# First three projections of a layer cut into two contraction halves, with their weights loaded before the second half of the modulation weights

## The chip, the core and the metric

The kernel runs on one core of one Trainium2 chip. The metric is the device time of one execution in microseconds. Three runs of the kernel before gave 792.9, 792.96 and 793.29 us, so their median is 792.96 us. The engines are named as in the profile: PE is TensorE (PEld its weight loads), DVE is VectorE, ACT is ScalarE, POOL is GpSimd, SP is SyncE, which here only issues the big transfers. All data is 32-bit floating point.

## The reference, cut to what matters

Two layers, each on 128 context tokens and 128 latent tokens of width 1024. The part that the change touches is the beginning of a layer:

```
m = silu(cond) @ w_mod + b_mod            # 6 x 1024 values per condition: shift, scale, gate, ...
h = rmsnorm(x, g_mix) * (1 + scale) + shift
aq, ak, av, mq, mk, mv, mo, mi, mf = split(h @ w_in)      # one combined input projection
group A: bidirectional mLSTM from mq, mk, mv, gates mi, mf, output gate mo
group B: grouped-query attention from aq, ak, av
x = x + gate1 * (concat(attention, mLSTM) @ w_out)
x = x + gate2 * moe(rmsnorm(x, g_ffn) * (1 + scale2) + shift2)   # 16 experts, 512 wide
```

Shift and scale of a feature need all 1024 rows of w_mod, but only the columns of that feature. A projection sums over all 1024 features of h (the contraction); the first 512 features are its first half.

## The kernel before, in words

Tokens lie transposed: a tile of h (hT) has 8 chunks k of 128 features, each with 256 columns, two blocks b of 128 tokens (block 0 context, block 1 latent). Every big weight arrives in pieces of 2 MB (1 MB for akv). They go round a ring of seven slots (ring), in the order of weight_plan(), and the experts use three slots more (beside, over). SP issues the transfers strictly in that order; before each it waits until the last user of the slot has read it (was_read). A wait of SP therefore holds back every later transfer. Small inputs are issued by ACT and POOL; POOL begins with them when the first projection weight (mk) has landed.

Within a layer the shift and scale of the first norm (section 0 of the modulation) are made first. In layer 0 section_rows multiplies four slots of w_mod, each two rows k of 2048 columns, on PE (L639, 16 recorded instructions for one slot); ACT copies the row (L1298), PE turns it (L651), DVE adds the bias and makes 1 + scale (L1591, L1598), and ACT and DVE apply it to the normed tokens (L1341, L1609). Then PE projects in the order mk, mq with the gate columns between its halves, mv, aq, scan and maximum rows, akv, mo (project L764, project_turned L778). A matmul of 512 columns is two recorded instructions.

Section 1 of the modulation (the gate of the mixer) isn't made on PE but summed on DVE: section_sums multiplies each of its four ring slots (blocks 0 to 3, in the file called ("mod", l, 1, i)) by the condition and adds it up (L1676, L1678), four instructions for each block. The table SUM_TURNS says how many blocks are summed at each of three turns: before the scan rows of the mLSTM, after the mq copies, and after gaps(0), the first half of the decay matrix (L1740). Before, layer 0 has three blocks in the first turn, one in the second, none in the third. PE reads the sums right after mo (L729). After that turn DVE empties akv out of PSUM (L1749, L1750), makes gaps(1), the q and k norms and the rotary (L1756 to L1782), the reciprocal of the output gate (L1787) and the weighted scores of the mLSTM (L1796), on which the first state-free matmuls of the mLSTM (own, L892) wait.

The experts follow: eight pairs of experts in a layer, 12 MB each, PE bound to the slots' landing (L1100 gate and up, L1130 down).

Of the kernel before, what the change touches and what calls it, by code (L numbers as in the profile page):

```python
# [105 lines left out]
SECTION_CHUNKS[1, 2], SECTION_CHUNKS[1, 3] = (32, 8), (40, 8)  # L106


def section_slots(l, s):

    return SECTION_CHUNKS[l, s][1] // 4
# [17 lines left out]
BETWEEN = {"mk": (0,), "mq": (1, 2), "mv": (3,)}  # L129
SUM_TURNS = (((0, 1, 2), (3,), ()), ((0, 1, 2), (3,), ()))  # L130


def bank_plan():
# [15 lines left out]
    put(("modrow", 0, 0), 7)  # L149
    put(("modcol", 0, 0), 7)  # L150
    for l in range(DEPTH):
# [10 lines left out]
        put(("gates", l), 4)  # L162
        for g in PROJ:
            for b in range(NB):
                turn((g, b))
        put(("gateT", l), 5)
# [69 lines left out]
def weight_plan():  # L236
# [13 lines left out]
    for i in range(section_slots(0, 0)):  # L250
        put(("mod", 0, 0, i))
    for l in range(DEPTH):
        for g in PROJ:
            put((g, l))
            for i in BETWEEN.get(g, ()):
                put(("mod", l, 1, i))
# [16 lines left out]
def build(nc, t):  # L273
    banks, weights = bank_plan(), weight_plan()
    with ExitStack() as ctx:
# [132 lines left out]
        first_read, last_half = sem("first_read"), sem("last_half")  # L408
        sum_step = sem("sum_step")
# [86 lines left out]
        def _(sp):  # L496
# [51 lines left out]
            load_section(0, 0, 0)  # L548
# [3 lines left out]
            load_section(0, 0, 1, 2, 3)  # L552
            for l in range(DEPTH):
                for g, (c0, width) in PROJ.items():
                    load((g, l), w_in[l, :, :, c0:c0 + width], width)
                    if g in BETWEEN:
                        load_section(l, 1, *BETWEEN[g])
# [53 lines left out]
        def _(pe):  # L611
# [33 lines left out]

            def section_columns(l, s):
# [64 lines left out]
            for l in range(DEPTH):  # L711
                bank = begin(("rows", l))
                done(("rows", l), pe.transpose(bank[:, 0:ROWS_L], rowsin[:, l, :], ident[0:ROWS_L, 0:ROWS_L]))
            pe.wait_ge(x_in, 16 * NB)
            for r in range(4):
# [5 lines left out]
                done(("x", r), mm)  # L721

# [10 lines left out]
            for l in range(DEPTH):  # L733
                if l == 0:
                    pe.wait_ge(cond_silu, 1)
                    section_rows(0, 0, 0)
                else:
                    warm((("mk", 0), l), 4)
                norm_parts(l, 0)
                if l == 0:  # L740
                    norm_parts(l, 1)
                    section_rows(0, 0, 1)
                norm_total(l, 0)
                if l == 0:
                    norm_total(l, 1)
                    section_rows(0, 0, 2, 3)
                    warm((("mk", 0), l), 3)
                    section_columns(0, 0)
                    warm((("mk", 0), l), 6)
                else:  # L750
# [4 lines left out]
                def project(g, which=range(NB), fresh=False):  # L755
                    _, width = PROJ[g]
                    w = landed((g, l))[:, 0:KD * width].rearrange("p (k n) -> p k n", k=KD)
                    for b in which:
                        bank = begin(((g, b), l))
                        for k in range(KD):  # L760
                            if fresh:
                                ready, n = (h_v, HV_STEPS) if k % 2 else (h_a, HA_STEPS)
                                pe.wait_ge(ready, n * l + 4 * b + k // 2 + 1)
# [4 lines left out]
                        done(((g, b), l), mm)  # L768

                def project_turned(g, which):  # L770

                    w = landed((g, l)).rearrange("p (k n) -> p k n", k=KD)
                    for i in which:
                        bank = begin(((g, i), l))
                        for j in range(2):
                            h = 2 * i + j
                            for k in range(KD):
                                mm = pe.matmul(bank[:, j * TOK:(j + 1) * TOK], w[:, k, h * MD:(h + 1) * MD], hT[:, k, :],  # L778
                                               start=(k == 0), stop=(k == KD - 1))
                        done(((g, i), l), mm)  # L780
# [46 lines left out]
                project("mk", fresh=True)  # L827
# [1333 lines left out]
```

## Time and profile before

| what | value |
|---|---|
| median of three runs | 792.96 us |
| profiled execution, its own time | 794.9 us |
| span in it | 793.0 us |
| PE busy | 759.5 us, 96% |
| DVE busy | 329.3 us, 42% |
| ACT busy | 158.2 us, 20% |
| bytes moved | 289.41 MB, 365 GB/s over the span |
| granted clock, mean | 0.996 |

The profiled execution is 1.9 us longer than its span. Busy shares are a mean over stages: PE is busy nearly everywhere after the first projection starts, and transfers run at full rate except at the start, in a gap before layer 0's mixer ends and in one in layer 1. What counts for a change of the first stage is which wait ends last in it, and whether that time survives the later waits.

### The profile page before, as it was taken

How to read it: one execution, taken by the hardware profiler on the slowest of the kernel's cores; microseconds unless marked ns; L12 is line 12 of the kernel's file. 1: busy time of each engine (PE TensorE's matmuls, PEld its weight loads, DVE VectorE, ACT ScalarE, POOL GpSimd, SP SyncE). 2: the span in 40 equal slices, each digit the busy share in tenths (PEclk: the TensorE clock that was granted, in tenths of full speed). 3: DMA queues.
4: the chain of work that ended last, by engine and by line, in shares of the span. 5: the costliest groups of instructions: out<-in, count | busy, mean ns of one | idle time of the engine just before them, and what ended most of it. 6: DMA issues, size and time to landing. Idle time of an engine off the chain costs nothing.

```text
span 793.0 us, 10913 instructions
## 1 busy us (share of the span) xinstructions
PE 759.5 (96%) x4683; PEld 401.3 (51%) x4683; DVE 329.3 (42%) x534; ACT 158.2 (20%) x355; POOL 56.6 (7%) x69
## 2 busy tenths in 40 slices
PE   3799999999999999999899999999899999999997
PEld 2265556786534433444245646688653444344423
DVE  0279566714323232123228965772431323213223
ACT  2301114602212012020012111361221201102001
POOL 0040052101100000000000004200110000000000
PEclk9999999999999999999999999999999999999999
DMA  8999907999999999999999970579889999999993
GB/s 346 403 378 374 375 7 295 413 362 424 426 420 424 423 421 425 426 419 423 422 407 407 380 301 0 218 289 397 326 328 400 427 426 418 424 426 419 426 421 152
DMA packets 49858, 289.41 MB, mean 365 GB/s; under 512 B 3401, under 2 KB 5761, under 8 KB 23697
## 3 DMA queue, kind: packets, MB, share of 16 engines
q1 hardware_dynamic: 48080, 285.30, 88.6%
q0 software_dynamic: 1488, 3.31, 1.2%
q8 instruction: 39, 0.64, 0.3%
q10 hardware_dynamic: 240, 0.08, 0.0%
q14 instruction: 11, 0.08, 0.0%
HBM read 286.31 MB, written 2.37 MB: 364 GB/s over the span
## 4 chain that ended last, share of the span: by engine, by line
PE 83%; DMA 13%; DVE 2%; SPq 1%; ACT 1%; issue 0%; ACTq 0%; DVEq 0%
PE ps L1100 22%; PE ps L764 16%; PE ps L1130 12%; DMA ring<-in_w_e_up 9%; PE ps L1014 7%; PE ps L1084 4%; DMA ring<-in_w_in 4%; PE ps L778 4%; PE ps L639 3%; PE ps L1145 2%; PE ps L1112 1%; PE ps L1155 1%; PE ps L892 1%; PE ps L917 1%; PE ps L947 1%; DVE xT L1654 1%
## 5 line engine op out<-in xcount | busy, mean ns | idle before, releaser
L1100 PE MATMUL ps<-ring,xe 128*64 128x512 f32 x688 | 151.8, 594 | 4.0 <-DMA ring<-in_w_e_up 4.0
L764 PE MATMUL ps<-ring,hT 128*128 128x512 f32 (+1 forms) x320 | 128.7, 564 | 2.0 <-DMA ring<-in_w_in 2.0
L1100 PEld LDWEIGHTS ps<-ring,xe 128*64 128x64 f32 x688 | 48.5, 137 | 105.3 <-issue 99.8
L764 PEld LDWEIGHTS ps<-ring,hT 128*128 128x128 f32 x320 | 62.1, 196 | 65.2 <-issue 59.5
L1130 PE MATMUL ps<-ring,ex 128*32 128x512 f32 x736 | 92.0, 594 | 0.2 <-issue 0.2
L1995 DVE COPY ye<-ps 64x512 f32<-64x512 f32 (+1 forms) x28 | 19.3, 689 | 164.2 <-PE ps L1130 164.1
L1014 PE MATMUL ps<-hT,ring 128*128 128x256 f32 x256 | 57.1, 381 | 0.0
L1979 DVE RECIPROCAL ex<-ex 128x512 f32<-128x512 f32 x16 | 53.6, 3353 | 0.6
L1130 PEld LDWEIGHTS ps<-ring,ex 128*32 128x32 f32 x736 | 26.0, 110 | 52.1 <-issue 49.4
L1977 DVE TENSOR_SCALAR ex<-ex 128x512 f32<-128x512 f32 x16 | 6.8, 427 | 109.4 <-ACT ex L1528 109.4
L1014 PEld LDWEIGHTS ps<-hT,ring 128*128 128x128 f32 x256 | 48.0, 190 | 7.2 <-issue 0.8
L1100 PE MATMUL ps<-beside,xe 128*64 128x512 f32 x208 | 46.2, 594 | 0.0
L1528 ACT ACTIVATE ex<-ps 128x512 f32<-128x512 f32 x16 | 9.6, 597 | 143.4 <-PE ps L1100 143.4
L1130 PE MATMUL ps<-beside,ex 128*32 128x512 f32 x224 | 35.3, 594 | 2.0 <-issue 2.0
L1678 DVE SCALAR_TENSOR_TENSOR pT<-ring,cT,pT 128x2048 f32<-128x2048 f32 x14 | 32.9, 2348 | 5.6 <-DMA ring<-in_w_mod 5.6
L1678 DVE SCALAR_TENSOR_TENSOR sideways<-ring,cT,sideways 128x2048 f32<-128x2048 f32 x14 | 32.9, 2347 | 0.0
L1084 PEld LDWEIGHTS ps<-lists,hT 128*128 128x128 f32 x256 | 29.7, 192 | 5.8 <-issue 4.9
L639 PE MATMUL ps<-ring,cT 128*32 128x512 f32 (+1 forms) x320 | 31.6, 525 | 0.6 <-DMA ring<-in_w_mod 0.6
L1084 PE MATMUL ps<-lists,hT 128*128 128x128 f32 x256 | 31.6, 278 | 0.1
L1544 ACT ACTIVATE ye<-ps 64x512 f32<-64x512 f32 (+1 forms) x28 | 16.6, 592 | 68.7 <-PE ps L1130 68.6
L1521 ACT ACTIVATE xe<-ps 128x512 f32<-128x512 f32 x32 | 19.1, 597 | 54.0 <-PE ps L1084 54.0
L1100 PEld LDWEIGHTS ps<-beside,xe 128*64 128x64 f32 x208 | 14.6, 137 | 30.0 <-issue 29.9
(272 smaller groups left out, 803.6 us busy)
## 6 DMA issues: line engine op xcount, KB each, us to landing
ring<-in_w_mod SPq DMA_DIRECT2D x24, 2048.0 KB, 19.1
ring<-in_w_e_up SPq DMA_DIRECT2D x23, 2048.0 KB, 20.0
ring<-in_w_e_gate SPq DMA_DIRECT2D x20, 2048.0 KB, 22.3
ring<-in_w_e_down SPq DMA_DIRECT2D x19, 2048.0 KB, 23.2
ring<-in_w_in SPq DMA_DIRECT2D x10, 2048.0 KB, 23.4
beside<-in_w_e_gate SPq DMA_DIRECT2D x8, 2048.0 KB, 25.5
beside<-in_w_e_down SPq DMA_DIRECT2D x7, 2048.0 KB, 19.8
beside<-in_w_e_up SPq DMA_DIRECT2D x5, 2048.0 KB, 18.1
```

The lines of the kernel that those rows point to most:

```text
L639: mm = pe.matmul(bank[32 * g:32 * g + 32, 0:width], cT[:, c:c + 32], w[:, k, g * width:(g + 1) * width], start=(c == 0), stop=(c == NB * ( ...
L764: mm = pe.matmul(bank[:, 0:width], hT[:, k, b * P:(b + 1) * P], w[:, k, :], start=(k == 0), stop=(k == KD - 1))
L778: mm = pe.matmul(bank[:, j * TOK:(j + 1) * TOK], w[:, k, h * MD:(h + 1) * MD], hT[:, k, :], start=(k == 0), stop=(k == KD - 1))
L1014: mm = pe.matmul(bank[:, j * TOK:(j + 1) * TOK], w[:, k, c:c + P], cat[:, k, :], start=(k == 0), stop=(k == KD - 1))
L1084: mm = pe.matmul(bank[:, c:c + P], htok[:, b, 2 * i + k, :], pick[:, b, 4 * q:4 * q + 4, :].rearrange("p e c -> p (e c)"), start=True, sto ...
L1100: mm = pe.matmul(bank[PLACES * j:PLACES * j + PLACES, :], xe[:, k, c:c + PLACES], w[:, j, i, :], start=(k == 0), stop=(k == KD - 1))
L1130: mm = pe.matmul(bank[32 * g:32 * g + 32, :], hidT[:, k, c:c + SLOTS], w[j][:, k, half * 512:(half + 1) * 512], start=(k == 0), stop=(k == ...
L1521: act.activation(xe[:, 2 * i:2 * i + 2, :].rearrange("p k (e b s) -> p b (k e) s", e=4, b=NB), bank[:, :].rearrange("p (b n s) -> p b n s" ...
L1544: ins = act.activation(ye[r, plane, 0:512], bank[r, :], ACT.Copy)
L1678: ins = dve.scalar_tensor_tensor(modsum[b], w[:, k % 2, :], one, modsum[b], ALU.mult, ALU.add)
L1979: dve.reciprocal(ex[:, :], ex[:, :]).then_inc(silu_step, 1)
L1995: ins = dve.tensor_copy(ye[r, plane, 512:1024], bank[r, :])
```

## The change

Section 0 of layer 0 is cut by features: part -1 is shift and scale of features 0 to 511 (two slots, all 1024 rows of w_mod), part 0 those of features 512 to 1023. feature_rows multiplies a slot with 32 matmuls of 128 columns in place of 8 of 512. mk, mq and mv of layer 0 are loaded and multiplied in two halves of the contraction. Weights of the first halves stand ahead of part 0 of w_mod, and tokens and constants ahead of every weight. Section 1 of layer 0 is loaded behind akv and mo, its sums on DVE are taken as 1, 1 and 2 blocks. Projections keep their partial sums in PSUM between the halves (mv moved to banks 4 and 5, gates to 6, gateT to 7). POOL's small inputs start when the first half of mk has landed. The last scatter of layer 0's experts stands behind the branch for spilled tokens.

```diff
+HALVED = ("mk", "mq", "mv")
-BETWEEN = {"mk": (0,), "mq": (1, 2), "mv": (3,)}
-SUM_TURNS = (((0, 1, 2), (3,), ()), ((0, 1, 2), (3,), ()))
+BETWEEN = ({"akv": (0, 1), "mo": (2, 3)}, {"mk": (0,), "mq": (1, 2), "mv": (3,)})
+SUM_TURNS = (((0,), (1,), (2, 3)), ((0, 1, 2), (3,), ()))
...
+            load_features(-1)
+            for g, landed in zip(HALVED, front_in):
+                if weights[g, 0][0] == RING - 1:
+                    taken(sp, ("x", 0), ("x", 1), ("x", 2), ("x", 3))
+                load_rows(g, slice(0, KD // 2), landed)
+            load_features(0)
+            for g in HALVED:
+                load_rows(g, slice(KD // 2, KD), slot_landed[weights[g, 0][0]])
...
+            def feature_rows(s, *which):
+                bank = begin(("modrow", 0, s)) if 0 in which else ps[banks["modrow", 0, s][0]]
+                for v in which:
+                    w = landed(("mod", 0, s, v)).rearrange("p (k n) -> p k n", k=KD)
+                    for k in range(KD):
+                        for g in range(4):
+                            mm = pe.matmul(bank[32 * g:32 * g + 32, v * P:(v + 1) * P], cT[:, NB * k:NB * k + 32],
+                                           w[:, k, g * P:(g + 1) * P], start=(k == 0), stop=(k == KD - 1))
...
+            pe.wait_ge(ones_set, 3)
+            warm(("x", 0), 12)
             pe.wait_ge(const_in, 16)
-            pe.wait_ge(ones_set, 3)
-            pe.wait_ge(rows_in, 16 * ROW_LOADS * DEPTH)
...
+                    front, back = range(0, KD // 2), range(KD // 2, KD)
+                    project("mk", fresh=True, ks=front)
+                    project_turned("mq", range(NB), front)
+                    feature_rows(0, 0, 1)
+                    project("mv", (0,), ks=front)
+                    section_columns(0, 0)
+                    project("mv", (1,), ks=front)
+                    project("mk", fresh=True, ks=back)
+                    project_turned("mq", (0,), back)
+                    gates()
+                    project_turned("mq", (1,), back)
+                    gate_rows()
+                    project("mv", ks=back)
...
-                if l + 1 < DEPTH:
-                    scatter_pair(PAIRS - 1, 0, KD)
                 with pe.If(limit[0] > SLOTS):
...
-                if l + 1 == DEPTH:
-                    scatter_pair(PAIRS - 1, 0, KD)
+                scatter_pair(PAIRS - 1, 0, KD)
...
+                    taken(dve, (("ssq1", 1), l))
+                    scaled(sq, 1, 0, KD)
+                    dve.wait_ge(xr_ready, n + 3)
+                    for s in (-1, 0):
+                        feature_columns(s)
+                        for b in range(NB):
+                            modulate(l, sq, b, (4 * s + 5, 4 * s + 7))
...
-            pool.wait_ge(slot_landed[weights["mk", 0][0]], 16)
+            pool.wait_ge(front_in[0], 16)
```

In feature_rows the four values of g are the four strips of 32 rows of the PSUM bank; in a partial project_turned a matmul of zeros clears the bank first (L831 of the changed kernel), since two heads share it.

PE, before, from the first slot of w_mod to the first projection of layer 0 (ring holds the weights, cT the two conditions, hT the modulated tokens, ps a PSUM bank):

```order
L639 MATMUL ps<-ring,cT 32x512 x8
L676 MATMUL ps<-work,ones 32x128 x16
L639 MATMUL ps<-ring,cT 32x512 x8
L685 MATMUL ps<-rstd,ones 128x128 x2
L639 MATMUL ps<-ring,cT 32x512 x16
L691 MATMUL ps<-zeros 128x512 x3
L651 MATMUL ps<-cst,ring 128x128 x4
L691 MATMUL ps<-zeros 128x512 x6
L764 MATMUL ps<-ring,hT 128x512 x16
L778 MATMUL ps<-hT,ring 128x256 x16
```

PE, changed, from the second slot of part -1 on, with the semaphores that each group waits on:

```order
L685 MATMUL ps<-ring,cT 32x128 [waits slot_landed1]
L685 MATMUL ps<-ring,cT 32x128 x31
L697 MATMUL ps<-cst,ring 128x128 [waits bank_read7]
L818 MATMUL ps<-ring,hT 128x512 [waits h_a,bank_read0,mk_front_in]
L831 MATMUL ps<-zeros 128x512 [waits bank_read2,mq_front_in]
L836 MATMUL ps<-hT,ring 128x256 x8
L685 MATMUL ps<-ring,cT 32x128 [waits slot_landed2,bank_read7]
L685 MATMUL ps<-ring,cT 32x128 [waits slot_landed3]
L818 MATMUL ps<-ring,hT 128x512 [waits bank_read4,mv_front_in]
L818 MATMUL ps<-ring,hT 128x512 [waits bank_read5,mv_front_in]
L818 MATMUL ps<-ring,hT 128x512 [waits h_a,slot_landed4]
L836 MATMUL ps<-hT,ring 128x256 [waits slot_landed5]
```

Before the first projection PE now reads two slots of w_mod in place of four; the other two are read behind the front halves of mk and mq.

DVE, before, from the second turn of sums to the emptying of akv in layer 0 (pT and sideways hold the two running sums, W the decay matrix):

```order
L1678 SCALAR_TENSOR_TENSOR sideways<-ring,cT,sideways 128x2048
L1728 COPY qc<-ps6 128x64
L1740 TENSOR_SCALAR W<-ps4,qc 128x128 x4
L1740 TENSOR_SCALAR W<-ps5,qc 128x128 x4
L1749 COPY qk<-ps0 128x128
L1750 COPY vx<-ps0 128x2x64
L1740 TENSOR_SCALAR W<-ps6,qc 128x128 x4
```

DVE, changed, the same place:

```order
L1826 COPY qc<-ps6 128x64
L1838 TENSOR_SCALAR W<-ps5,qc 128x128 x4
L1776 SCALAR_TENSOR_TENSOR pT<-ring,cT,pT 128x2048 [waits sum_step,slot_landed5]
L1776 SCALAR_TENSOR_TENSOR sideways<-ring,cT,sideways 128x2048 [waits sum_step]
L1776 SCALAR_TENSOR_TENSOR pT<-ring,cT,pT 128x2048 [waits sum_step]
L1776 SCALAR_TENSOR_TENSOR pT<-ring,cT,pT 128x2048 [waits sum_step,slot_landed6]
L1847 COPY qk<-ps 128x128 [waits bank_full2]
L1848 COPY vx<-ps 128x2x64
```

Eight sums (two blocks of four, of which half are listed) now stand between gaps(0) and the emptying of akv, where none stood; the first turn has four in place of twelve.

## Rows read from the trace of the kernel before

**Rows 1.** The page: GB/s in 40 slices of 19.8 us

```profile
GB/s 346 403 378 374 375 7 295 413 362 424 426 420 424 423 421 425 426 419 423 422 407 407 380 301 0 218 289 397 326 328 400 427 426 418 424 426 419 426 421 152
```

**Rows 2.** The chain of waits in order of time: start us, us, what

```profile
5.35 28.75 DMA ring<-in_w_in
34.14 15.70 PE ps L764 x32
49.84 6.91 PE ps L778 x32
...
65.86 27.66 PE ps L764 x64
```

**Rows 3.** Timeline, 15 to 34 us: start us, us, engine, line, instructions, idle before

```profile
18.93 0.61 PE L676 MATMUL ps<-work,ones 128*32 128x128 f32 x16
...
27.48 1.92 PE L639 MATMUL ps<-ring,cT 128*32 128x512 f32 x16 [0.62 <-DMA ring<-in_w_mod]
...
31.31 1.65 ACT L1341 ACTIVATE hT<-work,modc,amp 128x128 f32<-128x128 f32 x4 [1.25 <-DVE amp L1598]
```

**Rows 4.** Stretches, PE alone: us, busy (instructions), granted clock, DMA share, GB/s

```profile
0.00:20.00 20.00, 7.77 (x50) 1.00 0.88 346
20.00:40.00 20.00, 15.80 (x91) 0.91 1.03 399
40.00:60.00 20.00, 20.00 (x82) 1.00 1.03 380
28.00:30.00 2.00, 2.00 (x19) 1.00 1.06 389
36.00:37.00 1.00, 1.00 (x2) 0.50 0.97 391
98.00:99.00 1.00, 1.00 (x4) 0.50 0.04 16
170.00:175.00 5.00, 5.00 (x30) 1.00 0.74 298
416.00:420.00 4.00, 4.00 (x30) 1.00 1.05 396
```

**Rows 5.** Timeline of DVE in layer 0's mixer

```profile
79.14 2.35 DVE L1678 SCALAR_TENSOR_TENSOR pT<-ring,cT,pT 128x2048 f32<-128x2048 f32 x1
81.41 2.35 DVE L1678 SCALAR_TENSOR_TENSOR sideways<-ring,cT,sideways 128x2048 f32<-128x2048 f32 x1
...
95.78 2.16 DVE L1740 TENSOR_SCALAR W<-ps,qc 128x128 f32<-128x128 f32 x8 [1.35 <-PE ps L822]
...
105.61 0.28 DVE L1750 COPY vx<-ps 128x128 f32<-128x128 f32 x1
...
117.17 0.83 DVE L1782 TENSOR_TENSOR qkr<-work 128x640 f32<-128x640 f32 x1
122.45 0.19 DVE L1591 TENSOR_TENSOR modc<-ps,cols 128x32 f32<-128x32 f32 x1 [4.44 <-PE ps L651]
...
125.94 2.42 DVE L1796 TENSOR_TENSOR W<-ps,W 128x512 f32<-128x512 f32 x4
```

**Rows 6.** Timeline of PE in layer 0's mixer

```profile
93.46 0.71 PE L811 MATMUL ps<-cst,prob 64*128 64x64 f32 x8
...
130.81 1.38 PE L892 MATMUL ps<-mv,W 128*128 128x129 f32 x10
```

**Rows 7.** Waits of SP, 140 to 215 us: us in total, times, longest

```profile
SPq L576 <- DMA out_new_state_n<-nst: 20.4, 1, 20.4
```

**Rows 8.** Timeline of POOL, 150 to 210 us

```profile
165.01 0.53 POOL L2113 DMA_DIRECT2D out_new_state_n<-nst  x1
```

**Rows 9.** Timeline of PE, end of layer 0's experts

```profile
377.47 7.07 PE L1130 MATMUL ps<-beside,ex 128*32 128x512 f32 x64 [1.99 <-issue]
...
392.42 3.65 PE L1100 MATMUL ps<-ring,xe 128*64 128x512 f32 x16 [0.86 <-DMA ring<-in_w_e_up]
397.29 3.22 PE L1100 MATMUL ps<-ring,xe 128*64 128x512 f32 x14 [1.22 <-DMA ring<-in_w_e_up]
```

More of the change, by code:

```diff
@@ L161, in bank_plan @@
         put((("ssq1", 1), l), 5)
-        put(("gates", l), 4)
+        put(("gates", l), 6 if l == 0 else 4)
         for g in PROJ:
             for b in range(NB):
-                turn((g, b))
-        put(("gateT", l), 5)
+                if l == 0 and g == "mv":
+                    put((("mv", b), 0), 4 + b)
+                else:
+                    turn((g, b))
+        put(("gateT", l), 7 if l == 0 else 5)
         put(("scanT", l), 6)
@@ L248, in put @@
         order.append(slot)
-    for i in range(section_slots(0, 0)):
-        put(("mod", 0, 0, i))
+    for s in (-1, 0):
+        for i in range(section_slots(0, s)):
+            put(("mod", 0, s, i))
+    for g in HALVED:
+        put((g, 0))
     for l in range(DEPTH):
         for g in PROJ:
-            put((g, l))
-            for i in BETWEEN.get(g, ()):
+            if l > 0 or g not in HALVED:
+                put((g, l))
+            for i in BETWEEN[l].get(g, ()):
                 put(("mod", l, 1, i))
@@ L551, in _, with load_features, load_rows @@
                 sp.dma_start(xtok[:, b, :], t[name][0]).then_inc(x_in, 16)
[L552 removed]
+            def load_features(s):
+                for i in range(section_slots(0, s)):
+                    slot, _, _ = weights["mod", 0, s, i]
+                    c = KD * P * i + WB * (s + 1)
+                    sp.dma_start(ring[:, slot, :].rearrange("p (k n) -> p k n", k=KD), w_mod[0, :, :, c:c + WB]).then_inc(slot_landed[slot], 16)
+            def load_rows(g, ks, landed):
+                c0, width = PROJ[g]
+                sp.dma_start(ring[:, weights[g, 0][0], :].rearrange("p (k n) -> p k n", k=KD)[:, ks, :],
+                             w_in[0, :, ks, c0:c0 + width]).then_inc(landed, 16)
+            load_features(-1)
[4 more added lines that the diff above has]
+            load_features(0)
+            for g in HALVED:
+                load_rows(g, slice(KD // 2, KD), slot_landed[weights[g, 0][0]])
             for l in range(DEPTH):
                 for g, (c0, width) in PROJ.items():
[L555 to L557 removed]
+                    if l > 0 or g not in HALVED:
+                        load((g, l), w_in[l, :, :, c0:c0 + width], width)
+                    if g in BETWEEN[l]:
+                        load_section(l, 1, *BETWEEN[l][g])
                 for sec in later_sections(l)[1:-1]:
@@ L721, in _ @@
                 done(("x", r), mm)
+            pe.wait_ge(rows_in, 16 * ROW_LOADS * DEPTH)
+            for l in range(DEPTH):
+                bank = begin(("rows", l))
+                done(("rows", l), pe.transpose(bank[:, 0:ROWS_L], rowsin[:, l, :], ident[0:ROWS_L, 0:ROWS_L]))
             def section_sums(l, s):
```

127 lines of the change are left out of this document (80 added, 47 removed).

## The prediction

> **What bounds the kernel now.** I read the page's slices first, then the chain of waits, then the timelines of the stretches that the chain crosses. The transfers run at 346 to 425 GB/s for most of the span, with a hole at 99 to 119 us (7 GB/s) and one in layer 1 [rows 1]. The chain begins with a transfer: the wait for the first projection weight lasts 28.75 us, mk starts on PE at 34.14, and from there the chain stays on PE through mk, mq, mv, aq [rows 2]. So the first 34 us are bound by bytes, and behind them PE is bound by its own work. PE's later idle time that a transfer ends is 1.99, 0.86 and 1.22 us at the end of layer 0's experts, 4.1 together [rows 9]: PE and the transfers run nearly level there, which matters for what survives of an early start. The hole at 99 to 119 us shows that a start of PE some microseconds earlier meets weights that can also come earlier.
>
> **The sum is made against the profiled execution**: span 793.0, own time 794.9 us, 1.9 above the median 792.96. Each term below is a shift, negative for earlier, and carries over to the median unchanged.
>
> **Term 1, the start of mk.** Before, the fourth slot of w_mod landed at 27.48 [rows 3]. Asked for by then were four slots of 2.10 MB, 1.05 MB of tokens and 0.15 of constants and rows, 9.6 MB; moved were 20 us x 346 GB/s + 7.48 us x 399 = 9.9 MB [rows 4]. For mk, landed at 34.14 with 11.7 MB asked for, 12.6 were moved. So landing lags the queue by 0.3 to 0.9 MB. Changed: constants, tokens and two slots are 5.4 MB, with the lag 5.7 to 6.3 MB, which counted back from 6.92 MB at 20 us with some 0.4 MB in a microsecond is 17.0 to 18.4; I take 18.0, since pieces of 2 KB are now the rule. Then the second slot's rows on PE. Their form isn't in the trace; the nearest is the norm's 32x128 matmul, 16 recorded instructions in 0.61 us, 0.57 when nothing overlaps at the end, 0.036 each [rows 3]. A slot is 32 matmuls or 64 instructions: 2.3 us (the 32x512 form of before took 1.92 for a slot [rows 3], that is the lower bound; twice the row, 4.6, the upper). End at 20.3. From the end of the last rows (29.40) to the first modulated chunk (31.31 + 0.41) before were 2.3 us, through copy, transposes, bias and scale [rows 3]; the same again gives 22.6, and the six zero matmuls behind the transposes fill PE to about 23.0. The first half of mk needs 6.4 + 0.9 = 7.3 MB, there at 21. The norm of both blocks goes through ACT before that: the tokens no longer stand behind 2.1 MB of weights and come some 5 us earlier, so it is hidden under the slots of w_mod. So mk starts at 23.0 in place of 34.14: **-11.1 us**.
>
> **Term 2, work added on PE before the end of mv.** The matmuls of the three projections stay the same in number. New behind the start of mk are the two slots of part 0, 2 x 2.3 = 4.6 us, their transposes 0.35, and two zero matmuls that clear the banks of mq, 0.25 each (a recorded instruction of a 512-column matmul takes 13.83 / 32 = 0.43, the upper bound): 5.45 us. Must PE wait for part 0? Asked for up to its second slot are 5.4 + 3 x 1.05 + 2 x 2.10 = 12.7 MB, with the lag 13.6, and with 0.6 MB of the small inputs, which now start at 21 in place of 34.14, 14.2 MB. At 399 GB/s that is 38.2 us, at 380 GB/s [rows 4] 39.2. PE wants the slot at 23.0 + 6.9 (half of mk) + 7.5 (half of mq, 6.91 to 7.1 [rows 2], and the clearing) + 2.3 = 39.7. No wait, but little room: every 5% of rate is 1 us. The back halves (1.05 MB each) land before 46, PE takes mk's at 49. Before, the granted clock was at the lower level (0.50, that is 1.2 GHz) soon after the start, as at 36 to 37 [rows 4], and mk took 15.70 us where 32 instructions of mv or aq take 27.66 / 2 = 13.83 [rows 2]: 1.9 us. I leave this loss in, as if the first heavy stretch always paid it. Shift at the end of mv and at the scan columns: -11.1 + 5.45 = -5.65, term 2 **+5.45 us**.
>
> **Term 3, sums on DVE.** Before, aq ended and the scan columns were at 93.46, gaps(0) on DVE at 95.78 to 97.9, akv copied by 105.9 [rows 5, 6]. Changed, eight sums of 2.26 us (81.41 - 79.14) stand behind gaps(0): 18.1 us, then the four copies at 1.0: 19.1 in place of 8.0, so DVE is 11.1 us later against PE. Their slots land in time: SP issues them as mq and mv are read, near 64 and 72, and they are wanted at 90 and 99. Behind the sums are queued akv's copies, gaps(1), norms, rotary, the reciprocal and the weighted scores, for which PE waits with own. What slack has that queue? 4.44 us idle before L1591, which waited for PE, and between the first half of the weighted scores (125.94 + 1.21) and own at 130.81 another 3.66 [rows 5, 6]: 8.1. 11.1 - 8.1 = **+3.0 us** for PE. Bounds: 0 if the queue closes up elsewhere (the POOL squares and ACT's root are asked for later than before), 11.1 if no slack can be used. In the same stretch ACT copies the modulation row only behind the q and k roots; PE reaches it at 112.6, waits about 3 us, and that wait is part of the same 3.0, not more.
> The first turn has four sums in place of twelve. It ends when the first block has landed (about 61) and 7.0 us later, at 68, level with the logarithm that the scan waits for (PE's gate rows end near 65), and aq, 13.8 us on PE, covers the scan either way: 0.
>
> **Term 4, the queue before the experts.** SP waited 20.4 us for new_state_n, issued by POOL at 165.01 and landed 9.1 later [rows 7, 8]; meanwhile the queue ran dry for a while (298 GB/s, 0.74 busy at 170 to 175) [rows 4]. Changed, six slots (section 2 and w_out) can load before the modulation's columns are turned, where before three could; fewer bytes are then left over in front of the experts. Three slots of experts' weights wait behind new_state_n, 6.3 MB or 16 us of transfer, which before ran to about 190 and would now start while the queue is empty and end before PE frees the next slot: I put the lead at 1.6 us on top of the shift, of the 4.1 which PE lost to transfers at the end of the experts [rows 9]. **-1.6 us**, bounds 0 and -4.1.
>
> The scatter behind the branch: layer 1 has it in this order and starts it without a gap, 0. The zero matmuls at the very start stand ahead of the tokens, when PE has nothing to do: 0.
>
> Sum: -11.1 + 5.45 + 3.0 - 1.6 = -4.25. Span 788.75, own time 790.65, on the scale of the median **788.7 us**.
>
> **A rule on the clock.** At 416 to 420 mk of layer 1 starts right behind zero matmuls at the granted 1.00, while mk of layer 0 started behind 2 us of idleness and fell to 0.50 soon after [rows 4]. The Trainium skill says, in TensorE: Matmul & The Clock Gate, section Part 1: The HAM clock gate, that the half rate is the resting state and steady work releases it; by that rule the changed start, filled with zero matmuls to its last microsecond, keeps the full rate. The row at 98 to 99 (0.50 in the middle of dense work [rows 4]) goes against so simple a reading. Its result is the first rival.
>
> **A rule on pieces.** w_mod's pieces become 2 KB in place of 8 KB; while mk, also of 2 KB pieces, landed, the rate was 389 GB/s at a DMA share of 1.06, against 399 over the whole 20 us [rows 4]. The Trainium skill, DMA: Bandwidth & Descriptors, section Specifications, gives 512 B as enough for full rate, so by it the smaller pieces cost nothing; by the row, 3% of the 8 MB or 0.6 us, of which only the first half is on the path.
>
> **The rivals.**
> 1. No low clock at mk: 1.9 us less, 786.8; with the whole 4.1 of term 4 as well, 784.3. For it: the zero matmuls up to the start. Against: the 0.50 at 98.
> 2. The 4.44 us of DVE's slack can't be used, because the columns of the modulation slip with ACT's queue and DVE still waits for them: -4.25 + 4.44 = +0.2, 793.2. Or less: a new low clock (1.9) in PE's 3 us of waiting and no lead in term 4 (1.6): 792.2. For it: ACT's row copy stands behind DVE's reductions. Against: DVE itself reaches the columns at 121.8, by my times 5 us after PE has turned them.
> 3. Slower: the eight sums set PE's pace in full. Place: between gaps(0) and own in layer 0. Price 11.1 with no slack at all: -5.65 + 11.1 - 1.6 = +3.85, 796.8. It decides once more than 8.1 + 4.25 = 12.3 us of delay reach own, or the slack is under 3.9. For it: a chain over DVE, POOL, ACT and back. Against: the idle rows.
> 4. Small inputs and short pieces make part 0 late: each microsecond behind 39.7 costs one; 44 is break-even. It would take 300 GB/s between 20 and 44; the slices there say 374 and more [rows 1]. It widens the range only.
>
> **Chances.** Forecast (787.7 to 790.8) 0.42; rival 1 0.30; rival 2 0.18; rivals 3 and 4 0.10. A measurement here tells 0.2% (1.6 us) from no change, so faster means under 791.4: 0.42 + 0.30 + a quarter of rival 2 = 0.76; same 0.15; slower 0.09. Range 785.0 to 792.8; the likeliest case alone, 787.7 to 790.8.
>
> **What the changed profile would show.** mk starts at 22 to 24.5, and 64 instructions of the new row form take 2 to 3 us. No wait over 1 us before part 0. Scan columns at 87 to 89. DVE without a gap from gaps(0) to the weighted scores, and PE idle 2 to 4 us between mo and own. own at 127 to 129. Waits at the experts' end under 3 us. I would be wrong if mk started after 26, if PE waited for DVE by more than 6 us, or if the shift at own didn't reach the end of the span.

## The result: slower, and the profile after

| | before | changed |
|---|---|---|
| median | 792.93 us (792.17 to 793.29, 4 runs) | 800.5 us (799.67 to 801.25, 4 runs) |
| profiled execution | 794.9 us, span 793.0 | 799.67 us, span 797.9 |
| granted clock, mean | 0.996 | 0.99 |

The ratio is 1.0093, 95% interval 1.008 to 1.0106. The prediction was 788.7 us, faster; the kernel became 7.6 us slower. The two profiled executions stand 4.9 us apart (the one of before lies 2 us above its median, that of the changed kernel is the fastest of its four), so positions below explain 4.9 of the 7.6. Most of the other 2.7 lies in the profiled execution of before. Experiment 12 (the kernel before with one scatter moved) runs the same code up to the end of layer 0's experts, and its profile shows that code at the higher clock:

```profile
33.60 14.00 PE L764 MATMUL ps<-ring,hT 128*128 128x512 f32 x32 [1.81 <-DMA ring<-in_w_in]
...
92.06 0.71 PE L811 MATMUL ps<-cst,prob 64*128 64x64 f32 x8
...
127.73 2.06 PE L892 MATMUL ps<-mv,W 128*128 128x129 f32 x16
```

```profile
98.00:99.00 1.00, 1.00 (x6) 1.00 0.00 0
```

There mk takes 14.00 us, not 15.70, akv and mo (the last L764, 64 instructions) 20.91, not 22.59, and the weighted matmuls of the mLSTM (own) start at 127.73, not 130.81. Against this profile the changed kernel's first w_out matmul comes 7.2 us late (161.88 to 154.65), close to the 7.6 of the medians. Experiment 1, whose PE code is also that of before, takes 14.00 and 20.91 too. So one profile in three was at the lower clock at these two places, and that execution is the base of the prediction and of its rows. What decided it no run shows: zero matmuls and a wait of 1.7 to 2.0 us stand ahead of mk in all three. Below, "against the undisturbed profile" means against experiment 12 up to the first w_out matmul.

The start did what it should. PE timeline of the changed kernel, from the second slot of part -1 to part 0 (start us, us, engine, line, out<-in, instructions, idle before and what ended it):

```profile
19.52 1.96 PE L685 MATMUL ps<-ring,cT 128*32 128x128 f32 x64 [0.60 <-DMA ring<-in_w_mod]
...
23.63 7.11 PE L818 MATMUL ps<-ring,hT 128*128 128x512 f32 x16
...
38.00 1.96 PE L685 MATMUL ps<-ring,cT 128*32 128x128 f32 x64
41.23 0.97 PE L685 MATMUL ps<-ring,cT 128*32 128x128 f32 x28 [1.27 <-DMA ring<-in_w_mod]
```

mk starts at 23.63 where it started at 34.14 [rows 2], the new row form takes 1.96 us, and part 0 waits for 1.27. The start itself varies: in eleven profiles of kernels that share it, mk starts at 23.2 to 25.7, while the scan columns come at 86.8 to 87.7 in all of them. The trouble is on DVE. Its timeline, first turn of sums to the third:

```profile
65.97 1.29 DVE L1774 TENSOR_SCALAR pT<-ring,cT 128x2048 f32<-128x2048 f32 x1 [17.16 <-DMA ring<-in_w_mod]
...
73.15 0.42 DVE L1788 SCALAR_TENSOR_TENSOR prob<-prob 64x256 f32<-64x256 f32 x1
...
88.25 2.34 DVE L1776 SCALAR_TENSOR_TENSOR sideways<-ring,cT,sideways 128x2048 f32<-128x2048 f32 x1
90.51 0.21 DVE L1826 COPY qc<-ps 128x64 f32<-128x64 f32 x1
92.08 2.20 DVE L1838 TENSOR_SCALAR W<-ps,qc 128x128 f32<-128x128 f32 x8 [1.35 <-PE ps L882]
94.19 2.34 DVE L1776 SCALAR_TENSOR_TENSOR pT<-ring,cT,pT 128x2048 f32<-128x2048 f32 x1
```

DVE waits 17.16 us for the first block, and from 65.97 it works nearly without a gap: scan, second turn to 90.5, qc, gaps(0), third turn. PE's scan columns are ready at 87.9, and PE waits for qc:

```profile
87.18 0.71 PE L871 MATMUL ps<-cst,prob 64*128 64x64 f32 x8
90.87 2.31 PE L882 MATMUL ps<-prob,cst 32*128 32x256 f32 x16 [2.99 <-DVE qc L1826]
...
128.57 0.63 PE L947 MATMUL ps<-cst,qkr 128*128 128x128 f32 x4 [3.43 <-DVE qkr L1880]
...
133.31 3.69 PE L967 MATMUL ps<-mv,W 128*128 128x129 f32 x16 [0.86 <-DVE W L1894]
```

Here the scan columns answer to L811 and own to L892 of [rows 6]: 93.46 became 87.18, but 130.81 became 133.31 (92.06 and 127.73 in the undisturbed profile), with 3.43 us of waiting for the turned queries and keys and 0.86 for the weighted scores in front. Between them the end of DVE's queue:

```profile
112.29 0.28 DVE L1847 COPY qk<-ps 128x128 f32<-128x128 f32 x1
...
113.09 2.15 DVE L1838 TENSOR_SCALAR W<-ps,qc 128x128 f32<-128x128 f32 x8
...
117.32 4.03 DVE L1859 TENSOR_TENSOR qkr<-qk,qk_r 128x640 f32<-128x640 f32 x2 [0.63 <-ACT qk_r L1375]
...
124.14 1.61 DVE L1877 TENSOR_TENSOR work<-qkr,cst 128x160 f32<-128x160 f32 x4
125.79 2.64 DVE L1880 TENSOR_TENSOR qkr<-work 128x640 f32<-128x640 f32 x1
128.35 0.18 DVE L1668 TENSOR_TENSOR modc<-ps,cols 128x32 f32<-128x32 f32 x1
128.56 3.35 DVE L1885 RECIPROCAL og<-og 128x512 f32<-128x512 f32 x1
131.83 2.42 DVE L1894 TENSOR_TENSOR W<-ps,W 128x512 f32<-128x512 f32 x4
```

L1880 is L1782 of [rows 5]: 0.83 us became 2.64. The 4.44 us of idleness before modc are gone, as forecast. POOL meanwhile:

```profile
115.38 5.28 POOL L2192 TENSOR_TENSOR W<-W,cst 128x1024 f32<-128x1024 f32 x2
...
124.07 1.67 POOL L2195 TENSOR_SCALAR og<-og 128x512 f32<-128x512 f32 x1
125.56 2.18 POOL L2200 TENSOR_TENSOR kw<-mk,qc 128x512 f32<-128x512 f32 x2
```

kw runs beside L1880; before, kw came at 121.29, when DVE was idle. Stretches of the changed kernel, PE alone (from:to, length in us, PE busy (instructions), granted clock, DMA share, GB/s):

```profile
4.00:24.00 20.00, 15.07 (x199) 0.91 1.03 382
28.00:40.00 12.00, 11.96 (x105) 1.00 1.04 357
92.00:96.00 4.00, 4.00 (x16) 0.57 0.50 211
132.00:136.00 4.00, 3.14 (x18) 0.50 1.01 420
```

In the same stretches before, 4 to 24 and 28 to 40, transfers ran at 417 and 393 GB/s. The granted clock stays at the higher level under mk (1.00 at 28 to 40). That isn't shown to be a gain of the change, since the undisturbed profile has 1.00 there too, against 0.50 at 36 in [rows 4]. It is at the lower level behind each of the two long waits for DVE, but a wait isn't its only companion: in the profiled execution of before it was 0.50 at 98 behind 0.41 us of waiting.

### The profile page after: what moved, and what is told of

Read it like the earlier page. It is cut to its first block, busy times and chain, and to the rows that moved or that the text cites. A ratio compares the mean times of both kernels' runs of the same rounds, so it can differ in the third digit from the quotient of the medians.

```text
span 797.9 us, 11328 instructions
## 1 busy us (share of the span) xinstructions
PE 765.4 (96%) x4882; PEld 408.9 (51%) x4889; DVE 332.2 (42%) x536; ACT 157.4 (20%) x356; POOL 57.4 (7%) x69
## 4 chain that ended last, share of the span: by engine, by line
PE 73%; DMA 12%; DVE 9%; SPq 2%; issue 2%; ACT 1%; ACTq 0%; DVEq 0%
PE ps L1175 22%; PE ps L1205 12%; PE ps L818 10%; DMA ring<-in_w_e_up 9%; PE ps L1089 7%; PE ps L1159 4%; DMA ring<-in_w_mod 3%; PE ps L836 3%; PE ps L671 2%; PE ps L1220 2%; DVE pT L1776 2%; DVE sideways L1776 2%; SPq L573 1%; PE ps L967 1%; PE ps L1187 1%
## 5 line engine op out<-in xcount | busy, mean ns | idle before, releaser
L818 PE MATMUL ps<-ring,hT 128*128 128x512 f32 (+1 forms) x320 | 127.1, 556 | 0.0
L818 PEld LDWEIGHTS ps<-ring,hT 128*128 128x128 f32 x320 | 61.0, 193 | 61.4 <-issue 58.7
L1175 PEld LDWEIGHTS ps<-beside,xe 128*64 128x64 f32 x208 | 14.6, 137 | 30.0 <-issue 29.9
L2187 POOL TENSOR_TENSOR qkr<-qk 128x640 f32<-128x640 f32 x4 | 5.0, 1250 | 341.9 <-DVE vx L1848 341.9
## 6 DMA issues: line engine op xcount, KB each, us to landing
ring<-in_w_e_gate SPq DMA_DIRECT2D x20, 2048.0 KB, 23.3
ring<-in_w_e_down SPq DMA_DIRECT2D x19, 2048.0 KB, 23.2
```

Of the source, the lines that this page charges most:

```text
L818: mm = pe.matmul(bank[:, 0:width], hT[:, k, b * P:(b + 1) * P], w[:, k, :], start=(k == 0), stop=(k == KD - 1))
L1175: mm = pe.matmul(bank[PLACES * j:PLACES * j + PLACES, :], xe[:, k, c:c + PLACES], w[:, j, i, :], start=(k == 0), stop=(k == KD - 1))
```

## The experiments

Each ratio is against runs of the kernel before on the same chip, with its 95% interval. Times of different experiments come from different chips, so the ratios compare better. The theory throughout: the summing turns make DVE late, and PE pays. The rivals were the transfers, POOL beside DVE, and the clock.

**1. The table alone.** The kernel before with one line changed:

```diff
-SUM_TURNS = (((0, 1, 2), (3,), ()), ((0, 1, 2), (3,), ()))
+SUM_TURNS = (((0,), (1,), (2, 3)), ((0, 1, 2), (3,), ()))
```

> The kernel before with layer 0's sums taken as 1, 1 and 2 blocks, nothing else. Theory (the sums behind gaps(0) and what DVE and POOL do to each other behind them cost more than the start gave): akv copied near 117 in place of 106, own near 136 in place of 130.8, 3 to 8 us slower, 796 to 801. Rival (the loss comes from the new start and the transfers, DVE's slack of 8.1 takes the sums as far as forecast): own at most 3 us later, 793 to 796.

799.79 us, ratio 1.0101 (1.0082 to 1.0121). One line of the change, without the early start, costs what the whole change costs. DVE and PE there:

```profile
119.83 3.99 DVE L1761 TENSOR_TENSOR qkr<-qk,qk_r 128x640 f32<-128x640 f32 x2 [0.63 <-ACT qk_r L1303]
...
128.27 2.64 DVE L1782 TENSOR_TENSOR qkr<-work 128x640 f32<-128x640 f32 x1
```

```profile
131.06 0.93 PE L872 MATMUL ps<-cst,qkr 128*128 128x128 f32 x4 [1.94 <-DVE qkr L1782]
...
135.79 2.03 PE L892 MATMUL ps<-mv,W 128*128 128x129 f32 x16 [0.34 <-DVE W L1796]
```

The same two long instructions, the same two waits, and one more, of 1.64 us for ACT's og at 120. own is 5.0 us later than in the profile before, 8.1 later than in the undisturbed one, which fits the 7.5 us of the medians.

**2. The third turn made cheap.** In the changed kernel layer 0's third turn works on 64 of its 2048 columns, so part of the mixer's gate is left out; the transfers stay. The akv and mo of the next two expectations are one stretch on PE, L818 with 64 instructions.

```diff
+                                c = slice(0, 64 if l == 0 and which == SUM_TURNS[0][2] else 2048)
-                                    ins = dve.scalar_tensor_tensor(modsum[b], w[:, k % 2, :], one, modsum[b], ALU.mult, ALU.add)
+                                    ins = dve.scalar_tensor_tensor(modsum[b][:, c], w[:, k % 2, c], one, modsum[b][:, c], ALU.mult, ALU.add)
```

> The changed kernel with the eight sums of layer 0's third turn on 64 of 2048 columns (leaves out most of two blocks of the sum). Theory: DVE is free at gaps(1) when akv comes, own comes near 125, 7 to 10 us less than the changed kernel, 790.5 to 793.5. Rival (sums aren't the cause): under 3 us less.

793.51 us, ratio 1.0011 (1.0 to 1.0023): 6.5 to 7 us of the change's cost are back. What keeps it from the forecast is the wait for qc, which stands ahead of the third turn and is still there, with the lower clock behind it (3.78 us for what takes 2.00 at the higher, then 23.50 for akv and mo in place of 20.91); own comes at 129.99 where 125 was expected:

```profile
91.06 3.78 PE L882 MATMUL ps<-prob,cst 32*128 32x256 f32 x16 [3.02 <-DVE qc L1827]
```

**3. Second and third turn made cheap.** As 2, with more of the gate left out:

```diff
+                                c = slice(0, 64 if l == 0 and which != SUM_TURNS[0][0] else 2048)
```

> The changed kernel with the sums of layer 0's second and third turns on 64 of 2048 columns (leaves out most of three blocks of the sum). In the run with only the third turn short, PE still waited 3.0 us for DVE at 91, the maximum rows and akv and mo then took 1.8 and 2.7 us more than at the full clock. Theory (DVE's late second turn makes that wait, and the clock falls behind it): no wait at 91, akv and mo at 20.8, own near 124, 786 to 788. Rival (the clock falls there whatever happens): only the 3 us go, 789.5 to 791.

788.59 us, ratio 0.995 (0.9934 to 0.9965).

```profile
88.31 2.00 PE L882 MATMUL ps<-prob,cst 32*128 32x256 f32 x16 [0.41 <-DVE qc L1827]
...
122.86 2.06 PE L967 MATMUL ps<-mv,W 128*128 128x129 f32 x16
```

The wait for qc and the low clock behind it are gone, as the theory says, though 788.59 lies a little outside its 786 to 788 and below the rival's 789.5. own stands 8.0 us earlier than in the profile before and 4.9 earlier than in the undisturbed one; the medians differ by 4.4. So the early start is worth 4 to 5 us once DVE is out of the way. The two later turns cost 10.5 us at own (133.31 against 122.86) and 12 in the medians: 7 by the third turn (experiment 2) and 5 by the second, which ends too late for qc.

**4. kw held back.** POOL starts kw only behind the rotary, so that it doesn't run beside L1880:

```diff
                 taken(pool, ("scanT", l), (("mk", 0), l))
+                pool.wait_ge(qk_ready, NB * l + 2)
```

> The changed kernel with POOL's weighted keys (kw) held until both blocks of q and k are ready. Theory (DVE's last instruction of the rotary took 2.64 us in place of 0.83 because POOL computed beside it): it is back at 0.83, own 1.8 us earlier, 798.5 to 799. Rival (its length comes from elsewhere): 2.6 us stays, 800 to 801.

797.02 us, ratio 1.0054 (1.0037 to 1.0071).

```profile
126.92 0.82 DVE L1880 TENSOR_TENSOR qkr<-work 128x640 f32<-128x640 f32 x1
```

```profile
127.89 0.63 PE L947 MATMUL ps<-cst,qkr 128*128 128x128 f32 x4 [1.62 <-DVE qkr L1880]
...
132.63 2.02 PE L967 MATMUL ps<-mv,W 128*128 128x129 f32 x16 [1.92 <-DVE W L1894]
```

L1880 is back at 0.82 and PE's wait for it at 1.62 in place of 3.43, but the wait for the weighted scores grew from 0.86 to 1.92, and own came only 0.7 us earlier, since the whole queue was 1.1 later here (akv's copies at 113.42). The time fell more than expected because own's first group took 2.02 us, at the higher clock, where it had taken 3.69. So POOL's company costs the changed kernel some 3 us by the medians; 1.8 of it is L1880 itself, and the rest goes with the clock, which this run doesn't separate.

**5. Blocks loaded earlier, turns 2, 1, 1.** The edit names mk, mq, mv and aq in place of akv and mo. But the back halves of mk, mq and mv are issued by a loop of their own ahead of that table, so blocks 0, 1 and 2 all stand behind the back half of mv, and block 3 behind aq:

```diff
-BETWEEN = ({"akv": (0, 1), "mo": (2, 3)}, {"mk": (0,), "mq": (1, 2), "mv": (3,)})
-SUM_TURNS = (((0,), (1,), (2, 3)), ((0, 1, 2), (3,), ()))
+BETWEEN = ({"mk": (0,), "mq": (1,), "mv": (2,), "aq": (3,)}, {"mk": (0,), "mq": (1, 2), "mv": (3,)})
+SUM_TURNS = (((0, 1), (2,), (3,)), ((0, 1, 2), (3,), ()))
```

> The changed kernel with section 1's four slots of layer 0 loaded one each behind mk, mq, mv and aq, and the sums as 2, 1 and 1 blocks. Theory: the first block lands before 55, the scan chain begins by 69, the third turn has 9 us in place of 18, own near 126, 788 to 792. Rival (the order of loads only moves the wait to aq or akv): PE waits for a projection weight and the time stays above 796.

794.87 us, ratio 1.0033 (1.0018 to 1.0049), short of the 788 to 792 expected. Block 0 was there at 57.56, not before 55, and the first turn now sums two blocks, so the scan got no sooner (73.78) and the wait for qc stayed. own came at 129.4:

```profile
91.51 2.98 PE L882 MATMUL ps<-prob,cst 32*128 32x256 f32 x16 [3.38 <-DVE qc L1826]
```

**6. Long pieces.** The four slots of w_mod's section 0 in layer 0 are read in pieces of 8 KB, as before; the columns are then other ones, so the modulation isn't the reference's.

```diff
-                    sp.dma_start(ring[:, slot, :].rearrange("p (k n) -> p k n", k=KD), w_mod[0, :, :, c:c + WB]).then_inc(slot_landed[slot], 16)
+                    sp.dma_start(ring[:, slot, :].rearrange("p (k n) -> p k n", k=2), w_mod[0, :, 2 * i:2 * i + 2, 0:4 * WB]).then_inc(slot_landed[slot], 16)
```

> The changed kernel with the four slots of layer 0's section 0 read from the same amount of data in pieces of 8 KB (takes the wrong columns of w_mod). Theory (2 KB pieces cost bandwidth): the rate between 4 and 24 us returns from 370 to 389 to some 415 GB/s, mk starts about 1.5 us earlier, the first block of the sums lands 1 to 2 us earlier, total 1 to 2 us less. Rival (piece size costs nothing): all as in the changed kernel.

797.86 us, ratio 1.0074 (1.005 to 1.0099): 1.5 us less loss than the change's by the middle values, though the two intervals overlap. mk didn't start 1.5 us earlier, as expected, but at 24.68, within the spread of that start. The rates rise from 382 and 357 to

```profile
4.00:24.00 20.00, 15.32 (x195) 0.74 1.02 404
28.00:40.00 12.00, 12.00 (x79) 1.00 1.02 380
```

and the first block lands 2.0 us sooner (DVE at 63.96), which leaves 1.41 of the 2.99 us of PE's wait for qc. Short pieces lower the rate, then, but don't make the result.

**7. Small inputs later.** POOL begins with the small inputs when all of mk has landed, as before:

```diff
-            pool.wait_ge(front_in[0], 16)
+            pool.wait_ge(slot_landed[weights["mk", 0][0]], 16)
```

> The changed kernel with POOL's small inputs begun when all of mk has landed, in place of its first half. Theory (the small inputs are only a part of what slows 28 to 40 us): the second slot of part 0 lands about 1 us earlier, so PE's wait of 1.27 before it goes, total within 1.5 us of the changed kernel. Rival (they are the reason for the late first block): that block lands 4 us earlier, total 3 us less.

806.1 us, ratio 1.017 (1.0154 to 1.0185). The transfers ran at 385 GB/s at 28 to 40, not 357, still with short pieces, and the first block lands sooner (63.50), so the small inputs are a part of its lateness. But the scan now waits for the inputs themselves:

```profile
78.90 0.23 DVE L1786 TENSOR_SCALAR gqk<-gqk 128x128 f32<-128x128 f32 x1 [8.35 <-DMA brt<-in_b_router]
```

```profile
96.89 2.50 PE L882 MATMUL ps<-prob,cst 32*128 32x256 f32 x10 [8.52 <-DVE qc L1826]
```

Neither theory nor rival foresaw that. It is a dose of the same cause all the same: qc 6 us later than in the changed kernel, and the time 6 us longer.

**8. All of it together: a kernel that is faster.** The start stays; blocks 0 and 1 of section 1 load between the back halves of mk, mq and mv, blocks 2 and 3 behind mv and aq, turns 2, 1, 1 as in experiment 5, kw held back as in 4. Beyond those edits:

```diff
-            for g in HALVED:
+            for i, g in enumerate(HALVED):
                 load_rows(g, slice(KD // 2, KD), slot_landed[weights[g, 0][0]])
+                if i < 2:
+                    load_section(0, 1, i)
...
-                    if g in BETWEEN[l]:
+                    if g in BETWEEN[l] and (l > 0 or g not in HALVED[:2]):
```

> The changed kernel with section 1's first two blocks loaded between the back halves of mk, mq and mv, the third behind them, the fourth behind aq; sums as 2, 1 and 1 blocks; POOL's weighted keys behind q and k. Theory: first block lands near 50, first turn over by 68, second by 87 before PE's scan columns, third by 100, own at 124 to 125.5, 786 to 789 us. Rival (PE's gain is given back to transfers or to the clock at another place): 790.5 to 793.

788.69 us (787.53 to 789.98, 5 runs), ratio 0.9953 (0.9939 to 0.9966): 3.7 us faster than before by the ratio and some 11 than the change (11.8 between the medians of two chips).

```profile
51.62 1.29 DVE L1776 TENSOR_SCALAR pT<-ring,cT 128x2048 f32<-128x2048 f32 x1 [2.96 <-DMA ring<-in_w_mod]
...
69.25 0.42 DVE L1790 SCALAR_TENSOR_TENSOR prob<-prob 64x256 f32<-64x256 f32 x1
...
87.77 0.22 DVE L1828 COPY qc<-ps 128x64 f32<-128x64 f32 x1 [1.07 <-PE ps L873]
```

```profile
88.14 2.00 PE L884 MATMUL ps<-prob,cst 32*128 32x256 f32 x16 [0.41 <-DVE qc L1828]
...
122.69 2.06 PE L969 MATMUL ps<-mv,W 128*128 128x129 f32 x16
```

Block 0 is there at 51.62, the scan starts at 69.25 (before: 70.83), and DVE waits for PE at qc, not PE for DVE. No wait behind it, no low clock. own stands 5.0 us ahead of the undisturbed profile before.

**9. The same with kw at its old place.**

```diff
-                pool.wait_ge(qk_ready, NB * l + 2)
```

> The kernel called covered with POOL's weighted keys back at their old place. In it DVE reached the rotary at 114, with 0.82 for its last instruction, and waited for nothing behind. Theory (once DVE isn't behind PE, what POOL does beside it costs nothing): same as covered within 1 us, 788 to 790. Rival (POOL beside DVE costs wherever it is): 1.5 to 2 us more.

788.27 us, ratio 0.9947 (0.9926 to 0.9968), own at 123.0. The last instruction of the rotary took 2.64 us again, and nothing came later: where DVE isn't late, POOL's place doesn't matter. This kernel differs from experiment 5 only in the loads: block 0 stands two transfers earlier and block 1 one. By the ratios that is worth 6.8 us; between the two profiles 3.0 are the wait for qc and 3.3 the low clock behind it (L882 and akv and mo took 26.2 us there, 22.9 here).

**10. The same with the change's turns.** Kernel 8 with its loads:

```diff
-SUM_TURNS = (((0, 1), (2,), (3,)), ((0, 1, 2), (3,), ()))
+SUM_TURNS = (((0,), (1,), (2, 3)), ((0, 1, 2), (3,), ()))
```

> The kernel called covered with the sums as 1, 1 and 2 blocks, its early loads kept. Theory (the 2 blocks of the third turn are a cost of their own, near that of the kernel before with 1, 1, 2): 9 us later at gaps(1), of which PE's slack takes 4 to 5, and POOL beside DVE some more: own 4 to 7 us later, 792 to 796. Rival (only the late first block did the harm): under 1 us more than covered.

794.97 us, ratio 1.0034 (1.0015 to 1.0053): 6.3 us for one table, with early blocks and no wait for qc.

```profile
88.85 2.00 PE L884 MATMUL ps<-prob,cst 32*128 32x256 f32 x16 [0.41 <-DVE qc L1828]
...
129.41 3.57 PE L969 MATMUL ps<-mv,W 128*128 128x129 f32 x16 [1.91 <-DVE W L1896]
```

So a third turn of two blocks costs by itself, whatever lands when; one of one block, as in 8, lets own come at 122.69.

**11 and 12. The scatter.** Kernel 8 with layer 0's last scatter ahead of the branch, and the kernel before with it behind:

```diff
+                if l + 1 < DEPTH:
+                    scatter_pair(PAIRS - 1, 0, KD)
                 with pe.If(limit[0] > SLOTS):
```

> The kernel called covered with layer 0's last scatter ahead of the branch again. Theory (its place costs and gives nothing): within 0.7 us of covered. Rival (the branch's 0.7 us were hidden by the move): 0.7 us or more longer.

794.23 us, ratio 1.0018 (1.0006 to 1.0031), own unchanged at 123.0. I had expected 0.7 us at most; this takes back the whole gain of kernel 8 over the kernel before.

> The kernel before, with one edit: the last scatter of layer 0's experts stands behind the branch for spilled tokens, as in the changed kernel. Putting that scatter back ahead of the branch cost the covered kernel 5.9 us, as a 3.48 us wait that ended on nothing recorded and a stretch at a lower clock. Theory A (the order alone decides): the kernel before has a wait of that kind of only 0.72 us at this place, so the edit gives 0.5 to 1 us, 791.5 to 792.3, within what a measurement tells from no change. Theory B (the place of the branch costs several us in either kernel and the kernel before hides it): 787 to 790. Theory C (the cost depends on what else the program holds, its length ahead of the branch, and not on the scatter): 792 to 796, of either sign. I take A, 792.1.

796.89 us, ratio 1.0052 (1.0034 to 1.0071): 792.1 was expected, so theory A failed. PE in 11, in 12 and in kernel 8, one after the other:

```profile
409.93 1.07 PE L724 MATMUL ps<-work,ones 128*32 128x128 f32 x12 [3.48 <-issue]
```

```profile
411.34 3.79 PE L1155 MATMUL ps<-lists,ye 64*128 64x128 f32 x32 [3.50 <-issue]
```

```profile
402.42 2.06 PE L1232 MATMUL ps<-lists,ye 64*128 64x128 f32 x32
404.64 0.82 PE L739 MATMUL ps<-zeros 128*128 128x512 bf16 x3 [0.16 <-issue]
```

The cost sits in one wait of 3.5 us that ends on nothing recorded, with slower matmuls behind it. From the last down projection to mk of layer 1 it is 20.3 and 19.8 us in 11 and 12, against 14.5 in the kernel before, 14.5 in 8 and 14.6 in the change. The granted clock was 0.50 at 412 to 416 in both. Ahead of the branch is cheap in the kernel before (0.7) and dear in 8, behind it the other way about: neither order is the cause by itself. What is stays open; the expectation of 12 named a dependence on the rest of the program, and the signs fit that, but no run shows its mechanism. It doesn't disturb the other comparisons: from the first w_out matmul of layer 0 to mk of layer 1 the twelve other kernels take 260.1 to 260.5 us, those that leave out part of the sums or take other columns included, and 11 and 12 take 266.1 and 265.8. From there to the end it is 374.5 to 377.0, a spread that no experiment controls.

## Why the prediction was wrong, step by step

| step | forecast | against the profile before | against the undisturbed profile |
|---|---|---|---|
| 1: mk starts | -11.1 | -10.5 | -10.0 |
| 2: added work, scan columns | -5.65 | -6.3 | -4.9 |
| 3: gaps(0) on DVE | -5.65 | -3.7 | -2.3 |
| 3: gaps(1) on DVE | +5.45 | +7.3 | +10.4 |
| 3: end of the rotary on DVE | the same | +10.4 | +13.5 |
| 3: own on PE | -2.65 | +2.5 | +5.6 |
| first w_out matmul | -2.65 | +4.1 | +7.2 |
| 4: end of the span | -4.25 | +4.9 | (medians +7.6) |

**Term 1 held** to 0.6 us in this profile; in the eleven of that start it is up to 2 us less. **Term 2** was +4.2 for 5.45: part 0 did wait (1.27 against none), the new row form took 1.96 a slot in place of 2.3, and the loss of the low clock under mk, which I had left in, wasn't paid. That isn't rival 1 come true, since the kernel before doesn't pay it either in the two other profiles.

**That each shift carries over to the median unchanged was wrong too.** The profiled execution stood 1.9 us above the median, and its own low clock is part of the reason: 1.7 us under mk and 1.7 under akv and mo. The second of these stood inside the 8.0 us between gaps(0) and akv's copies that I subtracted in term 3; at the higher clock they are 6.3.

**Term 3 is the step that failed**, not in its large parts: the third turn lasted 18.1 us (94.19 to 112.29), as worked out, and the slack of 8.1 was there: the queue's +10.4 became +2.5 at own, 7.9 used up (the same 7.9 against the undisturbed profile). What failed is "the first turn: 0" and what the sum left out, here against the profile that I had:

- *The first turn.* Its block was to land at 61 and landed at 65.97. The scan began at 73.15 in place of 70.83, the second turn ended behind PE's need, gaps(0) began 3.7 us earlier than before where 5.65 were to be had: 1.9 us. The 61 had no working beside it. By its own numbers it would have done: from the scan to qc DVE takes 17.4 us, so with the scan at 68 qc would be read at 85.4, ahead of the scan columns at 87.9. My sentence left out that the second turn stands behind the scan and ahead of qc, and so did not see that only 2.5 us of room were there for a late block. The rate used them up: when the block landed, 23.3 MB had been moved, which the kernel before had reached at about 62 (314 GB/s over the first 20 us and 371 from there to 66, against 346 and 391).
- *POOL beside DVE.* The shifted queue met POOL's work: L1859 4.03 against 3.27, L1877 1.61 against 1.02, L1880 2.64 against 0.83, together 3.2, and the queue's delay grew from 7.3 to 10.4. The durations in my sum had been read where DVE stood alone, or, for the first, beside POOL for part of its length only. Experiment 4 shows the L1880 part: with kw later it is 0.82. The other two are read from overlap alone.

These two make 5.0 of the 5.15 us between -2.65 and +2.5; the slack (7.9 for 8.1) makes the rest. Against the undisturbed profile it is 8.2 us: 0.8 by the scan columns, 2.6 the first turn, 1.6 for the 6.3 in place of 8.0, 3.1 POOL and 0.2 the slack.

**The clock behind the waits** was in no term on this side. own's first group took 3.69 us where 16 instructions take 2.06, and by the first w_out matmul (161.97 against 157.83) the delay was 4.1: 1.6 more. I had priced a low clock only as half of rival 2. The Trainium skill says, in TensorE: Matmul & The Clock Gate, section Part 1: The HAM clock gate, that idleness brings the half rate back. The trace agrees here with 3.43 us of waiting and 0.50 behind it. The traces don't give a simple rule: in experiment 2 the wait for qc (3.02) was followed by 3.78 us for L882 and 23.50 for akv and mo, in the changed kernel (2.99) by 2.31 and 22.23, in experiment 4 waits of 1.62 and 1.92 by no low clock, and in the profile before 0.41 by 22.59 for akv and mo.

**Term 4 was worth nothing** (forecast -1.6): the waits at the experts' end were 1.26 and 1.23 us, against 0.86 and 1.22 [rows 9], and the delay stood at 4.0 to 4.1 from the projection of w_out to layer 1. Its upper bound of 4.1 was misread as well: the 1.99 in it ends on "issue" [rows 9], not on a transfer, so transfers ended only 2.1. The last 0.8 us came in layer 1; 0.67 of them is a wait ahead of its last scatter that ends on nothing recorded, and its cause is open.

The sum: 5.15 + 1.6 + 1.6 + 0.8 = 9.15 between -4.25 and +4.9; of the other 2.7 to the +7.6 of the medians, most is that the profiled execution of before was itself late.

**Of the rivals**, the third named the right place (the sums set PE's pace between gaps(0) and own) and the wrong price: it took the slack as unusable, while the slack was used and the load was greater. I gave it and the fourth 0.10 together. Its 12.3 us of delay was added up wrong: with the 3.0 of term 3 already in the forecast, it takes 8.1 + 3.0 + 4.25 = 15.35 us of added delay on DVE to lose the gain, and the runs had 16.7 (+10.4 against -6.3). The bound of term 3 that I kept, 11.1, was made only of the missing slack; nothing in it stood for instructions that get longer when they move, or for the clock behind a new wait. "PE waits for DVE by more than 6 us" was named as the sign that would prove me wrong: it was 2.99 + 3.43 + 0.86 = 7.3.

That 788.7 us is also what experiment 8 measures is no credit to the sum: it is another kernel.

## What to carry to other kernels

When work is pushed later in an engine's queue, read not only the slack behind it but every handover between its old and its new place; here qc stood between the second turn and the third, and PE paid there first. Take a second profile of the kernel before: one execution can hold a low clock that the others don't, and a term read from it then counts a loss that isn't there. A duration taken from the old place holds only with the old neighbours. And a load moved back to make room for an early start is due again at a definite instruction: place it by when the consumer's queue reaches it (4 MB of it moved one and two transfers forward were worth 6.8 us here).

## What the hardware showed beyond that

- DVE's instructions of two inputs grow when POOL computes beside them: 0.82 to 2.64 us beside kw, with the same operands. The Trainium skill, SBUF — State Buffer, section Who interferes with whom, says that a DVE instruction with two SBUF inputs contends with a GpSimd instruction that reads SBUF; experiment 4 agrees, since moving only POOL's instruction brings 0.82 back, and experiment 9 puts it in its old place and has 2.64 again.
- Pieces of 2 KB against 8 KB: 382 against 404 GB/s at 4 to 24 us and 357 against 380 at 28 to 40, in kernels that differ only in which part of w_mod four transfers read. All ten profiles with the short pieces have 376 to 384 GB/s at 4 to 24. The rest up to 417 before isn't explained. So the 512 B that the Trainium skill gives as enough (DMA: Bandwidth & Descriptors, section Specifications), weighed ahead of the result, isn't borne out here: 5 to 6% are missing. The small inputs cost about as much at 28 to 40: 357 with them, 385 with short pieces but without them in experiment 7.
- An "issue" wait of 3.5 us on PE near a branch appears or vanishes when code of the same work is put on its other side, in opposite directions in two kernels.
